# Second layer's down projection as seven block products, with weight blocks prepared during the first layer

## The chip, the cores and the metric

One core of one Trainium2 chip runs the whole kernel. The metric is the device time of one execution in microseconds (us). The kernel before was timed three times: 2796.79 to 2799.08 us, median 2798.24 us. Less is better. TensorE (PE) does the matrix products into PSUM, VectorE (DVE), ScalarE (ACT) and GpSimd (POOL) do elementwise work, SyncE (SP) issues the DMAs.

## The reference, cut to what matters

The reference is an encoder of two layers on 1024 positions of width 1024. Layer 0 has latent attention, layer 1 differential attention, and each ends with a gated MLP:

```
u = h @ w_up                       # 1024 -> 2 * 2816
u = conv over positions (width 3, depthwise) + bias
g, val = split(u)
x = x + (silu(g) * val) @ w_down   # 2816 -> 1024
```

After the second layer's MLP the output is `rmsnorm(x, final_norm_g)`. The change is about `(silu(g) * val) @ w_down` in both layers: in layer 1 its products change, and in layer 0 other work is set beside it. The weights `w_down` of both layers are inputs of the kernel.

## The kernel before, in words

**Layout.** Activations lie transposed: 128 features on the partitions, 1024 positions along the row. A matrix product of float32 accuracy is made of three TensorE passes over operands split into a high part (rounded to the engine's format) and a low part (the rest): high by high, high by low, low by high (`passes`). ACT makes a high part by a copy, POOL or DVE the low part by a subtraction. One matmul is 128 x 128 weights by 128 x 512 positions.

**The up projection** (`cycle` in each engine of `ffn_phase`) already works by seven block products, P1 to P7, of a 2 x 2 by 2 x 2 block scheme, for each of 22 pairs of tiles. Its result, the gated product y, goes tile by tile to DRAM (`ffn_products`), 22 tiles of 128 x 1024. The code names the last pair's products by `product_no(PAIRS - 1, ...)`.

**The down projection** (`project_down`, L1332 to L1334 for its passes) runs over 11 groups of two y tiles. In a group, TensorE makes 8 x 2 outputs (8 tiles of features, 2 halves of positions), each of 2 x 3 matmuls into one PSUM bank of eight (`DOWN_BANKS`, `NACC` = 8). It waits for the bank: output o needs the addition of output o - 8 (`acc_added`). DVE adds each output to the residual in SBUF (`add_down`, L1317). That is 176 outputs and 1056 matmuls in each layer. The fourth product of the last up pair (`fourth`) stands between the first two outputs.

**Order around it.** SP loads group g + 2 or later when the splits of a group have left the raw buffers (`fetch`). ACT's `step(g)` starts when group g - 2 is done on TensorE and splits two y tiles (`down_high_y`, L1129) and two weight tiles (`down_high_w`, L1134). POOL's `step(g)` makes the low parts (L1208, L1222). TensorE needs all of them for the group (`d_hi`, `d_lo`). Before the first group, SP loads the residual `x_out` from DRAM in eight DMAs (L1020), and DVE, after its last convolution and product of the up projection (`finish`), starts `add_down(0)`.

**End of layer 0.** In the last group, ACT and DVE also make the operands of the next layer's projections from the new residual: `unscaled_high` (L313) into `hh`, `unscaled_low` (L318) into `hl`, `unscaled_square` and `unscaled_add` for the norm, and `Ahead` loads and splits the first two weight tiles of the next phase. DVE's program has a `unscaled_low(m - 1)` behind the additions of tile m = 1, 2, 3, 4. A phase ends when all engines have come to its end.

**End of layer 1.** Each of the 16 additions of the last group is followed by a square on ACT (L1168), an addition of squares on POOL (L1235), and at the end a sum over partitions on TensorE (`norm_sum_halves`, L272): 12 matmuls of one column. Then DVE, ACT and DVE make the reciprocal root, and `final_norm_phase` scales and stores.

The engines' programs are written out by hand. Each engine runs its program in order. What holds it is the semaphore waits alone.

Of the kernel before, what the change touches and what calls it, by code (L numbers as in the profile page):

```python
# [18 lines left out]
F32 = mybir.dt.float32  # L19
# [6 lines left out]
P = 128  # L26
# [36 lines left out]
HX_AT = 28928  # L63
HX_HI_AT, HX_LO_AT = HX_AT, HX_AT + 56 * KB
# [768 lines left out]

def ffn_phase(nc, layer, x, x_out, x_dram, y_dram, up_dram, down_dram, vecs, cst, ones, nm, out_norm, unscaled, blocks, spaces,
              ahead):

    tag = f"ffn{layer}_"
    with ExitStack() as c:
# [59 lines left out]
        y_loaded = [sem(f"y_loaded{s}") for s in range(2)]  # L898
        down_loaded = [sem(f"down_loaded{s}") for s in range(2)]
        d_hi, d_lo = sem("down_hi"), sem("down_lo")  # L900
# [3 lines left out]
        last_use = [LastUse(d_hi, d_lo, 4 * (GROUPS - 1), acc_ready, lambda n: ADDS * (GROUPS - 1)) for s in range(2)]  # L904
# [7 lines left out]
        if unscaled:  # L912
            unscaled.squares_in(at("sq", [P, 3, SEQ], F32, RAW_AT), at("sq_more", [P, 3, SEQ], F32, PARTS_AT))
        else:
            sq = at("sq", [P, 3, SEQ], F32, RAW_AT)
            out_norm.sum_in(lambda k: x_out[:, k, :], [sq[:, 0, :], sq[:, 1, :]], sq[:, 2, :], ps[:, 0:QT],
                            sq_total=2 * KT)
# [50 lines left out]
        def _(sp):  # L968
# [14 lines left out]

            def load_down(g, s):
# [9 lines left out]
            def cycle(p, par, m):  # L994
                if is_last(p):
# [3 lines left out]
                    load_y(0, 0)  # L999
                    load_down(0, 0)  # L1000
# [15 lines left out]
            load_down(1, 1)  # L1016
            sp.wait_ge(prod, product_no(PAIRS - 1, "P5"))
            load_y(1, 1)
            for k in range(KT):
                sp.dma_start(x_out[:, k, :], x_dram[:, k, :]).then_inc(x_back[k], 16)  # L1020
            store_y(PAIRS - 1)
# [7 lines left out]
            with sp.Fori(1, (GROUPS - 1) // 2) as i:  # L1029
                fetch(2 * i, 0)  # L1030
                fetch(2 * i + 1, 1)
            fetch(GROUPS - 1, 0)
            if ahead:
                ahead.load(sp, last_use)

        @block.scalar
        def _(act):
# [43 lines left out]
            def cycle(p, par, m):  # L1081
# [22 lines left out]
                if is_last(p):  # L1104
                    down_high_y(0, 0, 1)
                need(act, prod, free(p, "A22"))
# [7 lines left out]
                if is_last(p):  # L1114
                    down_high_w(0, 0, 1)
                else:
# [25 lines left out]

            def step(g, s, m):
                if isinstance(g, int) and g == 0:
                    return
# [9 lines left out]
            if unscaled:  # L1155
# [2064 lines left out]
```

## Time and profile before

| | |
|---|---|
| median of three runs | 2798.24 us |
| profiled execution, its own time | 2799.92 us |
| its span | 2798.1 us |
| TensorE busy | 2715.1 us, 97% of the span |
| TensorE's mean granted clock | 0.991 |
| VectorE, ScalarE, GpSimd busy | 62%, 47%, 50% |
| DMA | 195.35 MB, mean 70 GB/s |
| down projection of layer 0 | 1159 to 1401 us of the span |
| down projection of layer 1 | from 2534 to 2775.7 us |

The profile gives one execution. Times are us from the start of the span. A matmul's own duration (about 390 ns in the rows) is longer than the distance to the next one, since matmuls overlap. The distance is what a matmul costs while TensorE has work.

### The profile page before, as it was taken

To read this page: it belongs to the slowest core of one execution; us is meant where nothing else is said; L and a number is where in the kernel's file an instruction comes from. 1 tells how busy PE (TensorE), PEld (TensorE's weight loads), DVE (VectorE), ACT (ScalarE), POOL (GpSimd) and SP (SyncE) were. 2 spreads that over 40 slices of the span, in tenths; PEclk is the share of its full clock that TensorE was granted. 3 is DMA by queue.
4 is the path that set the end of the run, shared out by engine and by line. 5 is a ranking of instruction groups with operands and counts; after the bars stand their busy time and mean duration, and the time that the engine had idled before them with its cause. 6 is when DMAs were issued, how large, how long until landed. Compare 5 with 4: busy or idle time off the path is not lost. (4 is left out here: it accounts for less than half of the span.)

```text
span 2798.1 us, 40653 instructions
## 1 busy us (share of the span) xinstructions
PE 2715.1 (97%) x13996; PEld 2263.8 (81%) x13996; DVE 1748.3 (62%) x2463; ACT 1314.0 (47%) x2035; POOL 1390.6 (50%) x1065
## 2 busy tenths in 40 slices
PE   8999999999989999999999999999898999999998
PEld 7788888887778888888878887887786888888886
DVE  6677777772764454555687777778428554455554
ACT  5577777772444444411245555555325444443112
POOL 1355555553687777644322222221247777775444
PEclk9999999999999999999999999999899999999999
DMA  3000000004122122522030000000321222125221
GB/s 140 23 11 10 7 7 7 18 1 160 51 91 90 68 90 90 203 91 105 30 115 31 31 31 31 31 23 23 158 106 38 90 90 86 71 105 196 95 85 60
DMA packets 54392, 195.35 MB, mean 70 GB/s; under 512 B 6545, under 2 KB 9873, under 8 KB 53777
## 3 DMA queue, kind: packets, MB, share of 16 engines
q1 hardware_dynamic: 54288, 193.95, 19.0%
q8 instruction: 68, 1.11, 0.2%
q14 instruction: 36, 0.29, 0.0%
HBM read 148.84 MB, written 45.09 MB: 69 GB/s over the span
## 5 line engine op out<-in xcount | busy, mean ns | idle before, releaser
L1332 PE MATMUL ffn_ps<-ffn_b,weights_hi 128*128 128x512 f32 x704 | 275.5, 391 | 11.7 <-ACT ffn_parts L1068 3.3
L1333 PE MATMUL ffn_ps<-ffn_b,weights_hi 128*128 128x512 f32 x704 | 274.4, 390 | 0.0
L1334 PE MATMUL ffn_ps<-ffn_b,weights_lo 128*128 128x512 f32 x704 | 274.4, 390 | 0.0
L1208 POOL TENSOR_TENSOR ffn_y_lo<-ffn_y_raw,ffn_y_hi 128x1024 fp32r<-128x1024 f32 x44 | 107.0, 2453 | 236.1 <-ACT ffn_y_hi L1129 236.1
L799 POOL TENSOR_TENSOR up_local_lo<-up_sums,up_local_hi 128x512 fp32r<-128x512 f32 x126 | 170.3, 1354 | 105.2 <-ACT up_local_hi L794 105.2
L409 POOL TENSOR_TENSOR weights_lo<-weights_raw,weights_hi 128x1024 fp32r<-128x1024 f32 (+2 forms) x64 | 124.4, 1949 | 192.6 <-ACT weights_hi L404 192.6
L2550 ACT ACTIVATE dif_p<-dif_s,dif_neg_max 128x1024 f32<-128x1024 f32 x128 | 142.4, 1115 | 143.3 <-DVE dif_neg_max L2755 143.3
L1332 PE MATMUL ffn_ps<-ffn_b,up_local_hi 128*128 128x512 f32 x504 | 196.3, 390 | 7.3 <-POOL up_local_lo L799 6.3
L1334 PE MATMUL ffn_ps<-ffn_b,up_local_lo 128*128 128x512 f32 x504 | 196.1, 389 | 0.0
L1333 PE MATMUL ffn_ps<-ffn_b,up_local_hi 128*128 128x512 f32 x504 | 196.1, 389 | 0.0
L1129 ACT ACTIVATE ffn_y_hi<-ffn_y_raw 128x1024 fp32r<-128x1024 f32 x44 | 44.2, 1051 | 315.0 <-PE ffn_ps L1334 315.0
L1317 DVE TENSOR_TENSOR x_second<-x_second,ffn_ps 128x512 f32<-128x512 f32 x176 | 120.3, 687 | 112.0 <-PE ffn_ps L1334 112.0
L2056 DVE TENSOR_REDUCE mat_row_max<-outer 128x1 f32<-128x1024 f32 x128 | 156.2, 1221 | 49.8 <-PE outer L420 48.1
L794 ACT ACTIVATE up_local_hi<-up_sums 128x512 fp32r<-128x512 f32 x126 | 78.9, 631 | 229.9 <-PE ffn_ps L1334 150.3
L1317 DVE TENSOR_TENSOR x_first<-x_first,ffn_ps 128x512 f32<-128x512 f32 x174 | 118.4, 686 | 103.9 <-PE ffn_ps L1334 103.9
L2755 DVE TENSOR_REDUCE dif_neg_max<-dif_s 128x1 f32<-128x1024 f32 x128 | 150.6, 1219 | 44.4 <-PE dif_s L2927 43.7
L1878 ACT ACTIVATE mat_pt_hi<-mat_turn 128x512 fp32r<-128x512 f32 x256 | 138.8, 594 | 79.0 <-PE mat_turn L2204 78.6
L1332 PEld LDWEIGHTS ffn_ps<-ffn_b,weights_hi 128*128 128x128 f32 x704 | 132.4, 188 | 42.9 <-issue 7.5
L1264 DVE SCALAR_TENSOR_TENSOR ffn_conv<-ffn_ps,vecs,ffn_conv 128x1023 f32<-128x1023 f32 x88 | 112.6, 1280 | 83.8 <-ACT ffn_conv L1053 83.8
L2073 DVE TENSOR_TENSOR mat_pt_lo<-mat_turn,mat_pt_hi 128x512 fp32r<-128x512 f32 x256 | 162.7, 677 | 2.3 <-ACT mat_pt_hi L1878 2.2
L1334 PEld LDWEIGHTS ffn_ps<-ffn_b,weights_lo 128*128 128x128 f32 x704 | 132.4, 188 | 27.6
L1333 PEld LDWEIGHTS ffn_ps<-ffn_b,weights_hi 128*128 128x128 f32 x704 | 132.4, 188 | 27.3
(420 smaller groups left out, 8169.4 us busy)
## 6 DMA issues: line engine op xcount, KB each, us to landing
weights_raw<-in_up SPq DMA_DIRECT2D x44, 512.0 KB, 3.7
up_raw<-in_up SPq DMA_DIRECT2D x44, 512.0 KB, 4.2
ffn_products<-ffn_conv SPq DMA_DIRECT2D x44, 512.0 KB, 2.6
ffn_y_raw<-ffn_products SPq DMA_DIRECT2D x44, 512.0 KB, 4.3
ffn_down_raw<-in_down SPq DMA_DIRECT2D x24, 512.0 KB, 6.8
weights_raw<-in_diff_qkv SPq DMA_DIRECT2D x23, 512.0 KB, 3.5
weights_raw<-in_down SPq DMA_DIRECT2D x20, 512.0 KB, 6.1
x_spill<-x_in SPq DMA_DIRECT2D x16, 512.0 KB, 3.9
```

The lines of the kernel that those rows point to most:

```text
L409: pool.tensor_tensor(w.lo[:], w.raw[:], w.hi[:].bitcast(F32), ALU.subtract).then_inc(w.lo_done, 1)
L799: pool.tensor_tensor(w.lo[name], w.block_raw(par, name), w.hi[name].bitcast(F32), ALU.subtract).then_inc(w.lo_done, 1)
L1264: dve.scalar_tensor_tensor(cv[:, 1:SEQ], pr[:, 0:SEQ - 1], vec(V_CONV_W + 2 * FT * 3 * layer, s, q), cv[:, 1:SEQ], ALU.mult, ALU.add).then ...
L1317: dve.tensor_tensor(xm, xm, bank(DOWN_BANKS[n % NACC]), ALU.add).then_inc(acc_added, 1)
L1332: pe.matmul(out, hi, x_hi, start=start, stop=False, skip_group_check=True)
L1333: pe.matmul(out, hi, x_lo, start=False, stop=False, skip_group_check=True)
L1334: return pe.matmul(out, lo, x_hi, start=False, stop=stop, skip_group_check=True)
L1878: act.activation(pt[:, 4 * half:4 * half + 4, (t % 2) * P:(t % 2 + 1) * P], turn_ps[half][:].rearrange("p (k m) -> p k m", m=P), ACT.Copy) ...
L2056: dve.tensor_reduce(row_max[:, col:col + 1], s_ps[t % 2][:], AX_X, ALU.max, negate=True).then_inc(max_ready, 1)
L2073: dve.tensor_tensor(pt_lo[b][part], turn_ps[half][:].rearrange("p (k m) -> p k m", m=P), pt_hi[b][part].bitcast(F32), ALU.subtract).then_i ...
L2550: act.activation((p0, p1)[m][t % 2][:], s_ps[m][:], ACT.Exp, bias=neg_max[:, col:col + 1], accum_out=total).then_inc(exp_done, 1)
L2755: dve.tensor_reduce(neg_max[:, col:col + 1], s_ps[m][:], AX_X, ALU.max, negate=True).then_inc(max_ready, 1)
```

## The change

**Layer 1, products.** The 22 y tiles are taken in six steps (`STEPS`): five of two pairs of tiles and one of one pair. In a step, the upper and the lower half of its tiles and the left and right half of the positions are the four blocks of y, and seven block products with seven blocks of weights replace the eight. A phase n of 42 is one product of one step; each makes four outputs q of `size` x 3 matmuls. TensorE's order is P1, P3, P2, P6, P5, P7, P4. POOL makes the four differences of y blocks (`difference`) and the low parts (`block_lo`), ACT the high parts (`block_hi`). DVE adds each output into the place of its kind of product (`place`): P1, P5, P6 have places of their own, the others lie in the residual. In the last step the places are combined (`combine`), 20 additions on DVE and 8 on POOL.

**Layer 1, weights.** They are not split there: SP loads the prepared high and low blocks of a phase, 512 KB each (half in step 1), in a ring of four (`load_weights`). In DRAM they lie by unit of 14 tiles, so a load takes runs of 1 KB.

**Layer 1, end.** 16 squares again. POOL adds ten of them into two, and TensorE sums these two and the last four: 24 matmuls.

**Layer 0.** Class `Prepare` makes the blocks in 11 rounds, one per group, of two units each. SP loads a unit's eight weight tiles in runs of 512 bytes, DVE makes four sums of 128 x 256, ACT the high part of 128 x 1792, POOL the low part of 128 x 1792, and SP stores both (0.92 MB each) and loads the next when the stores have landed. All of it stands in the engines' existing programs: DVE's sums of round 0 ahead of `add_down(0)`, those of round g + 1 in `add_down(g)` behind the additions of m = 3; ACT's and POOL's splits of round g at the end of `step(g)`; at the end ACT waits for all stores before its first `unscaled_high`.

The diff, cut:

```diff
+STEPS = ((0, 2), (4, 1), (6, 2), (10, 2), (14, 2), (18, 2))
+ORDER = ("P1", "P3", "P2", "P6", "P5", "P7", "P4")
+class Prepare:
+    def load(self, sp, g):
+        for j in range(2):
+            need(sp, self.stored[j], 32 * g)
+            for r in range(2):
+                for to, count, source in unit_source(self.source, 2 * g + j, r):
+                    sp.dma_start(self.raw[j][:, to:to + count, :], source).then_inc(self.loaded[j], 16)
+    def store(self, sp, g):
+        for j in range(2):
+            sp.wait_ge(self.lo_done, 2 * g + j + 1)
+            for z, part in enumerate((self.high[j], self.low[j])):
+                sp.dma_start(self.dest[2 * g + j, z], flat(part).bitcast(F32)).then_inc(self.stored[j], 16)
+    def sums(self, dve, g):
+        for j in range(2):
+            dve.wait_ge(self.loaded[j], 32 * g + 64)
+            dve.tensor_tensor(block(j, 8), block(j, 0), block(j, 4), ALU.subtract).then_inc(self.summed, 1)
+        for i, (to, a, b, op) in enumerate(...):      # three more for each j
+    def split_high(self, act, g):
+        for j in range(2):
+            act.wait_ge(self.summed, 8 * g + 7 + j)
+            act.activation(self.high[j][:], self.raw[j][:], ACT.Copy).then_inc(self.hi_done, 1)
+    def split_low(self, pool, g):
+        for j in range(2):
+            pool.wait_ge(self.hi_done, 2 * g + j + 1)
+            pool.tensor_tensor(self.low[j][:], ...)
...
 # SP, layer 0
             for k in range(KT):
                 sp.dma_start(x_out[:, k, :], x_dram[:, k, :]).then_inc(x_back[k], 16)
+            if prepare:
+                prepare.load(sp, 0)
             store_y(PAIRS - 1)
-            with sp.Fori(1, (GROUPS - 1) // 2) as i: ...
+            fetch(2, 0)
+            for g in range(GROUPS):
+                prepare.store(sp, g)
+                if g + 1 < GROUPS:
+                    prepare.load(sp, g + 1)
+                if g + 3 < GROUPS:
+                    fetch(g + 3, (g + 3) % 2)
+            ahead.load(sp, last_use)
+            prepare.all_stored(sp)
 # ACT, layer 0
             def step(g, s, m):
                 if isinstance(g, int) and g == 0:
+                    prepare.split_high(act, g)
                     return
...
                 down_high_w(g, s, m)
+                prepare.split_high(act, g)
             groups(act, step)
+            prepare.all_stored(act)
 # POOL, layer 0, end of step
+                prepare.split_low(pool, g)
 # DVE, layer 0
+                    if m == 3 and not end:
+                        prepare.sums(dve, g + 1)
...
             if unscaled:
+                prepare.sums(dve, 0)
+                groups(dve, lambda g, s, m: add_down(g))
                 return
 # DVE, layer 1
+            for n in range(PHASES):
+                s, name = n // 7, ORDER[n % 7]
+                last = s == len(STEPS) - 1
+                for q in range(4):
+                    o, to = 4 * n + q, place(name, q)
+                    if last and name == "P4":
+                        combine(to, place("P7", q), 5 + q)
+                        dve.wait_ge(combined, 17 + q)
+                    dve.wait_ge(acc_ready, o + 1)
...
+                if last and name == "P6":      # 8 combine
+                if last and name == "P5":      # 8 combine
 # PE, layer 1
+            for n in range(PHASES):
+                pe.wait_ge(weights_loaded[n % W_RING], 32 * (n // W_RING + 1))
+                pe.wait_ge(y_hi_done, n + 1)
+                pe.wait_ge(y_lo_done, n + 1)
+                for q in range(4):
+                    need(pe, acc_added, o - NACC + 1)
+                    for z in range(size):
+                        mm = passes(...)
+            pe.wait_ge(out_norm.sq_added, len(SQ_ADDED))     # ten
+            sum_squares(sq_part[:, 1, :], 1, first=True)
+            sum_squares(sq_part[:, 0, :], 0)
+            for n in range(2 * KT - 4, 2 * KT):
+                pe.wait_ge(out_norm.sq_ready, n + 1)
+                mm = sum_squares(sq_place(n), 0, final=n == 2 * KT - 1)
 # POOL, layer 1, last step
+                for q in range(4):
+                    pool.wait_ge(acc_added, last + 9 + q)
+                    pool.tensor_tensor(xm, xm, sum1[:, q, :], ALU.add).then_inc(c11_done, 1)
+                add_squares(SQ_ADDED[:6])
+                for q in range(4):
+                    pool.wait_ge(combined, 17 + q)
+                    pool.tensor_tensor(xm, xm, sum5[:, q, :], ALU.add).then_inc(c22_last, 1)
+                add_squares(SQ_ADDED[6:])
```

## Rows read from the trace of the kernel before

**Rows 1.** Page, busy time of each engine over the span.
```profile
PE 2715.1 (97%) x13996; PEld 2263.8 (81%) x13996; DVE 1748.3 (62%) x2463; ACT 1314.0 (47%) x2035; POOL 1390.6 (50%) x1065
```

**Rows 2.** Waits of PE, 1155 to 1405 us, then 2525 to 2798 us (total, times, longest).
```profile
PE dif_proj L418 <- PEq L3096: 2.5, 1, 2.5
...
PE fin_rstd L3032 <- PEq L3107: 1.6, 1, 1.6
PE ffn_ps L272 <- POOL ffn_sq L1235: 0.3, 1, 0.3
```

**Rows 3.** Timeline of DVE in layer 1's last group: start, us, instruction, idle before.
```profile
2766.26 0.69 DVE L1317 TENSOR_TENSOR x_second<-x_second,ffn_ps 128x512 f32<-128x512 f32 x1 [0.67 <-PE ffn_ps L1334]
2767.62 0.69 DVE L1317 TENSOR_TENSOR x_second<-x_second,ffn_ps 128x512 f32<-128x512 f32 x1 [0.67 <-PE ffn_ps L1334]
```

**Rows 4.** Timelines where layer 0's down projection begins: PE, SP, then DVE.
```profile
1159.03 0.39 PE L1332 MATMUL ffn_ps<-ffn_y_hi,ffn_down_hi 128*128 128x512 f32 x1
...
1163.11 0.39 PE L1332 MATMUL ffn_ps<-ffn_y_hi,ffn_down_hi 128*128 128x512 f32 x1
...
1157.64 4.18 SPq L1020 DMA_DIRECT2D x_first<-x_spill x8
...
1169.70 5.46 DVE L1317 TENSOR_TENSOR x_first<-x_first,ffn_ps 128x512 f32<-128x512 f32 x9
```

**Rows 5.** Timelines of ACT at two group starts, and of POOL for group 2's operands.
```profile
1183.79 2.01 ACT L1129 ACTIVATE ffn_y_hi<-ffn_y_raw 128x1024 fp32r<-128x1024 f32 x2 [14.76 <-PE ffn_ps L1334]
...
1205.46 2.01 ACT L1129 ACTIVATE ffn_y_hi<-ffn_y_raw 128x1024 fp32r<-128x1024 f32 x2 [17.77 <-PE ffn_ps L1334]
...
1184.93 4.78 POOL L1208 TENSOR_TENSOR ffn_y_lo<-ffn_y_raw,ffn_y_hi 128x1024 fp32r<-128x1024 f32 x2 [8.16 <-ACT ffn_y_hi L1129]
1189.67 4.74 POOL L1222 TENSOR_TENSOR ffn_down_lo<-ffn_down_raw,ffn_down_hi 128x1024 fp32r<-128x1024 f32 x2
```

**Rows 6.** Single lines: duration ns min/median/max, first and last start, form.
```profile
L1222 POOL TENSOR_TENSOR weights_lo<-weights_raw,weights_hi x20: 2386/2395/2422, 1172.0 to 2718.7; 128x1024 fp32r<-128x1024 f32 x20
L1235 POOL TENSOR_TENSOR ffn_sq<-ffn_sq x13: 1267/1292/1297, 2759.5 to 2775.8; 128x512 f32<-128x512 f32 x13
L1134 ACT ACTIVATE ffn_down_hi<-ffn_down_raw x20: 1042/1043/1048, 1150.2 to 2691.7; 128x1024 fp32r<-128x1024 f32 x20
L1168 ACT ACTIVATE ffn_sq<-x_second x16: 630/632/633, 2756.1 to 2776.5; 128x512 f32<-128x512 f32 x16
L2721 DVE TENSOR_TENSOR dif_rotated<-dif_rotated,dif_by_cos x32: 691/693/695, 1422.4 to 1933.6; 128x512 f32<-128x512 f32 x32
```

**Rows 7.** Page, DMA issues: KB each, median us from issue to landing.
```profile
ffn_products<-ffn_conv SPq DMA_DIRECT2D x44, 512.0 KB, 2.6
weights_raw<-in_mla_keys SPq DMA_DIRECT2D x8, 128.0 KB, 2.0
```

**Rows 8.** Windows: us, busy of PE, PEld, DVE, ACT, POOL, PEclk, DMA share, GB/s.
```profile
1170.00:1180.00 10.00, 10.00 (x46) 8.28 (x45) 7.53 (x13) 0.00 (x0) 6.77 (x3) 1.00 1.02 405
1227.30:1249.10 21.80, 21.80 (x98) 18.06 (x97) 11.04 (x17) 4.02 (x5) 9.48 (x4) 1.00 0.26 97
1379.50:1402.70 23.20, 21.77 (x97) 17.68 (x95) 20.36 (x22) 14.59 (x14) 5.76 (x2) 1.00 0.00 0
2778.00:2779.00 1.00, 1.00 (x6) 1.00 (x7) 0.00 (x0) 0.00 (x0) 0.00 (x0) 0.50 0.00 0
2779.00:2780.00 1.00, 1.00 (x5) 0.94 (x5) 0.00 (x0) 0.00 (x0) 0.00 (x0) 0.50 0.00 0
```

**Rows 9.** Timelines of DVE, ACT and POOL in layer 0's last group.
```profile
1385.59 3.07 DVE L318 SCALAR_TENSOR_TENSOR hl<-x_first,vecs,hh 128x1024 fp32r<-128x1024 f32 x1
...
1393.12 1.27 DVE L318 SCALAR_TENSOR_TENSOR hl<-x_first,vecs,hh 128x1024 fp32r<-128x1024 f32 x1
...
1382.99 1.15 ACT L313 ACTIVATE hh<-x_first,vecs 128x1024 fp32r<-128x1024 f32 x1 [19.78 <-DVE x_first L1317]
...
1385.17 5.76 POOL L409 TENSOR_TENSOR weights_lo<-weights_raw,weights_hi 128x1024 fp32r<-128x1024 f32 x2 [16.75 <-ACT weights_hi L404]
```

**Rows 10.** Timelines of PE and DVE where layer 1's down projection ends.
```profile
2775.35 0.39 PE L1334 MATMUL ffn_ps<-ffn_y_hi,ffn_last_lo 128*128 128x512 f32 x1
2775.84 1.05 PE L272 MATMUL ffn_ps<-ones,ffn_sq 128*128 128x1 f32 x8
2777.17 2.85 PE L272 MATMUL ffn_ps<-ones,ffn_sq 128*128 128x1 f32 x16 [0.28 <-POOL ffn_sq L1235]
...
2780.06 0.17 DVE L212 TENSOR_SCALAR final_norm_stat<-ffn_ps 128x8 f32<-128x8 f32 x1 [3.60 <-PE ffn_ps L272]
```

More of the change, by code:

```diff
@@ new lines, in quarter @@
+        def quarter(s, name):
+            size, buf = STEPS[s][1], tiles[s % 2]
+            upper, lower = buf[:, 0:size, :], buf[:, size:2 * size, :]
+            left, right = slice(0, HALF), slice(HALF, SEQ)
+            return {B11: upper[:, :, left], T3: upper[:, :, left], T1: upper[:, :, right], B21: lower[:, :, left],
+                    T4: lower[:, :, left], B22: lower[:, :, right], T2: lower[:, :, right]}[name]
+        BLOCK = {"P1": B11, "P3": B22, "P2": B21, "P6": T2, "P5": T1, "P7": T3, "P4": T4}
@@ L906, in b_part @@
+        LOWS = (0, T1, 1, T2, 2, T3, 3, T4, 4, 5, 6)
+        if prepared is None:
+            last_use = [LastUse(d_hi, d_lo, 4 * (GROUPS - 1), acc_ready, lambda n: ADDS * (GROUPS - 1)) for s in range(2)]
         def b_part(buf):
@@ L1112, in cycle @@
                     centre(1, p - 1, 1 - par)
-                if is_last(p):
+                if is_last(p) and prepared is None:
                     down_high_w(0, 0, 1)
+                elif is_last(p):
+                    block_hi(act, 1)
+                    block_hi(act, 2)
                 else:
@@ L1419, in project_down, with sum_squares @@
                         mm.then_inc(acc_ready, 1)
-            groups(pe, project_down)
             if unscaled:
+                groups(pe, project_down)
                 return
-            norm_sum_halves(pe, out_norm, ones, 2 * KT - 2, 2 * KT - 1)
+            for n in range(PHASES):
+                s, (hi, lo) = n // 7, parts_of(n)
+                size = STEPS[s][1]
+                pe.wait_ge(weights_loaded[n % W_RING], 32 * (n // W_RING + 1))
+                pe.wait_ge(y_hi_done, n + 1)
+                pe.wait_ge(y_lo_done, n + 1)
+                w_parts = weights[n % W_RING]
+                for q in range(4):
+                    o = 4 * n + q
+                    if o == 1:
+                        fourth(PAIRS - 1)
+                    if o in (2, 3, 4, 6):
+                        pe.wait_ge(*{2: (u2_done, PAIRS - 1), 3: (v_done, PAIRS - 1),
+                                     4: (conv_done[0], PAIRS), 6: (conv_done[1], PAIRS)}[o])
+                    need(pe, acc_added, o - NACC + 1)
+                    for z in range(size):
+                        mm = passes(bank(DOWN_BANKS[o % NACC]), w_parts[0][:, size * q + z, :], w_parts[1][:, size * q + z, :],
+                                    hi[:, z, :], lo[:, z, :], z == 0, z == size - 1)
+                    mm.then_inc(acc_ready, 1)
+            def sum_squares(squares, half, first=False, final=False):
+                for t in range(4):
+                    col = 4 * half + t
+                    mm = pe.matmul(out_norm.psum_sum[:, col:col + 1], squares[:, t * P:(t + 1) * P], ones[:, 0:1],
+                                   start=first and t == 0, stop=final and t == 3, skip_group_check=True)
+                return mm
+            pe.wait_ge(out_norm.sq_added, len(SQ_ADDED))
[4 more added lines that the diff above has]
+                mm = sum_squares(sq_place(n), 0, final=n == 2 * KT - 1)
+            mm.then_inc(out_norm.sq_summed, 1)
         return [bank(DOWN_BANKS[(2 * KT - 2 + half) % NACC]) for half in range(2)]
```

272 lines of the change are left out of this document (222 added, 50 removed).

## The prediction, made before the changed kernel was run

> **What bounds the kernel now.** I read the page's engine line first: TensorE is busy for 97% of the span [rows 1]. Then the waits of TensorE around both down projections: one wait of 2.5 us at a phase's start, 1.6 and 0.3 us at the end, and none inside [rows 2]. So here a matmul less is its distance to the next one less, and every other engine counts only where it makes TensorE wait. The distance: outputs of six matmuls follow each other every 1.36 us [rows 3], 0.227 us a matmul. A group of 16 outputs is 21.8 us, and ACT's group starts are 21.7 us apart [rows 5]. In such a group DVE has 11.0 us of work, ACT 4.0, POOL 9.5, the DMA a quarter of its time [rows 8]. That is the room into which layer 0 puts the preparation. But it has an order, and I follow that next.
>
> **Layer 1, TensorE.** The steps have sizes 2, 1, 2, 2, 2, 2, sum 11, and 7 products x 4 outputs x 3 passes: 924 matmuls in place of 1056. 132 x 0.227 = **-29.9 us**, if TensorE stays as full as now. DVE has 4 additions of 0.61 us (9 in 5.46 us, back to back [rows 4]) for a phase of 5.44 us, or 2.72 us in the small step: 2.44, just enough. POOL has per step 7 low parts and 4 differences of 2.4 us, 26 us of 38. A phase's weights are 1.05 MB, a step's tiles 2.1 MB: 9.5 MB in 38 us is 250 GB/s, and 405 GB/s were moved at a DMA share of 1 [rows 8]; the ring is three phases ahead, 16 us. Bounds 0 to +2 us for starved phases (the fourth weights stand behind the last y store, and land about when they are needed); I take 0. No row shows packets of 1 KB under load; see the rivals.
>
> **Layer 1, end.** Let T be the end of the last product, 2775.7 before; the column sums ended at T + 4.3 [rows 10]. In the last step DVE has, after P6's additions (T - 15.6), 8 combines, 4 additions, 8 combines, 4 additions, then four pairs of combine and addition: 32 instructions of 0.61 us, or 0.69 where one waits for the one before [rows 6]. That is T + 4.5, with no disturbance. The fourth c22 addition of POOL needs the last combine, T + 3.9, and behind it stand four additions of squares: 5 x 1.3 us [rows 6], so T + 10.4. TensorE waits for all ten additions before its first column sum. Then it has 24 matmuls where it had 12, recorded as 48 for 24. At half clock 11 records took 2 us [rows 8]: 48 take 8.7 us; at full clock 8 took 1.05 us: 6.3. The clock fell at about 2778, 2.3 us after the last product [rows 8, 10], and now TensorE does nothing for 10 us. DVE's combines read SBUF twice while POOL works. In the like place DVE's 128 x 1024 took 3.07 us while POOL was busy and 1.27 when it was not [rows 9]. I give each of the last four combines half a POOL instruction, +2.6 us. End T + 13 + 0.2 + 8.7 = T + 22: **+18 us**. Bounds: +12 (no disturbance, full clock) and +19 (each combine waits for a whole one).
>
> The Trainium skill, "SBUF — State Buffer", section "SBUF: two separate sides", says why: GpSimd and a DVE instruction with two SBUF inputs take a shared port in turn, whole instructions at a time. With it the end would be the upper bound, +19; the rows of 3.07 and 1.27 us agree with it.
>
> **Layer 0, start.** SP issues eight residual loads from 1157.6 to 1161.8, then, new, eight of 128 KB for round 0. The queue is full (share 1.02, 405 GB/s [rows 8]); 6.3 MB (two weight, two y, eight residual tiles) from 1155.5 last until 1171, and 1.05 MB more in runs of 512 bytes take 3.5 us (bounds 2.5 at the full rate, 5 at half). They land at about 1175.3. DVE used to start its additions at 1169.7 [rows 4]. Now it first waits for them and makes 8 sums of about 0.4 us (128 x 256; 0.69 for 512 [rows 6]): 3.2 us, so its first addition ends at 1179.2. TensorE needs it for the ninth output, at 1163.1 + 7 x 1.36 = 1172.6 [rows 4]: 6.6 us lost. Meanwhile ACT and POOL do round 0 before group 1. ACT: 128 x 1792 is 1.7 us (0.63 for 512, 1.04 for 1024 [rows 6]). POOL: 4.0 us (1.29 and 2.39 [rows 6]). The two low parts end at 1175.3 + 12.7 = 1188. Then POOL needs 9.5 us for group 1's operands [rows 5]: 1197.5. The stores of the second unit land 5.8 us after 1188: two of 0.92 MB are 4.5 us at 405 GB/s, and a store of 512 KB, landed in 2.6 us, has 1.3 beyond its transfer [rows 7]. Only then is the next load issued: 3.1 us (two issues, 1.8 as for the 128 KB loads [rows 7], 0.9 transfer). It lands at 1197, the sums end at 1200.1, and the addition of group 0's ninth output, which gives the next bank, at 1200.8. Group 1 starts at 1200.9, not 1183.7: **+17 us**. Bounds 14 and 20.
>
> **Layer 0, rounds.** Each round hangs on the one before: sums and splits 12.7, store 5.8, load 3.1, and 0.3 of wake-ups: 21.9 us, against TensorE's 21.8. Nothing of the eight banks' slack is left after group 1, so what a round takes above 21.8 is lost nine times. I take 22.6, since POOL, with 9.5 + 8.1 us a group, is often at work when DVE's sums come: **+7 us**. Bounds 21.8 (0; no gain, TensorE's own pace) and 25 (+29), with loads of 512 separate runs slow to issue or to land.
>
> The Trainium skill, "DMA: Bandwidth & Descriptors", section "Where 436 GB/s comes from", puts HBM traffic of a core at about 358 GB/s. By that estimate two stores and their loads would take 1 us longer and the sum 9 us more. The window above moved 405 GB/s, so the trace disagrees.
>
> **Layer 0, end.** Round 10's sums start 4 us before group 10 does, its stores land 18.6 us later: 14.6 us into the group. ACT waits for them before its first `unscaled_high`, which came 3.5 us into the group before [rows 8, 9]. DVE's `unscaled_low` behind m = 1 waits for that, and with it all later additions. Counting on (POOL's and ACT's splits of the next weights, queued behind the stores, come at 18.5, DVE has 10 additions, 4 lows of 1.27 and 3 additions of squares of 1.2 behind the first wait, and waits for ACT between them), DVE ends 32 us into the group, where it ended at 23.1: **+9 us**. Bounds +4 (stores early, by the free pace of DVE) and +11.
>
> **Sum.** -29.9 + 18 + 17 + 7 + 9 = +21. The profiled execution took 2799.92 us in all (span 2798.1), 1.7 above the median; on it 2821, and on the median of the runs, 2798.24, **2819 us**.
>
> **Rivals.** (a) *The rounds are hidden*: below 21.8 us a round, DVE's place behind m = 3 sets them; the stores of the last land about 9 us into group 10. +17 + 0 + 4 - 12 = +9, 2807 us. For it: the round is 21.9 by rows; against: no margin. (b) *The rounds are long*, 25 us: 17 + 29 + 10 - 12 = +44, 2842 us. For it: 512-byte runs of which no row exists, and the store, wait, load order; against: every piece is bounded by a row. (c) *Not slower*: the DMA engines deliver round 0's blocks before the residual, not behind it. Place: the first hole. Each us earlier than 1175 takes one off until DVE itself is free, 1169.7, and POOL then is done with group 1's operands at 1192 and the sums at 1194.7: the hole is 11.7 us. With (a) for the rest, 11.7 + 4 - 12 = +4, 2802 us, which no longer differs. It decides from a landing at about 1171. For it: the last residual load needs not be the last to land; against: full queue, later issue. All lower bounds together with it (end of layer 1 at +12) give -2, 2796 us. (d) *It does not do what it says*: weights in 1 KB packets at half the rate take 5.0 us and tiles 0.7 a phase, more than 5.44; TensorE would wait some 0.3 us a phase: 2830 us.
>
> **How the numbers follow.** Forecast 0.42, with a range of its own of 2809 to 2830; (a) 0.20, (b) 0.17, (c) 0.09, (d) 0.04; 0.08 remains for a gain that I don't see, down to the bare -30. From no change this kernel can be told by 0.2%, 5.6 us. Slower: forecast, (b), (d) and most of (a), 0.77; same: (c) and the rest of (a), 0.13; faster 0.10. The range 2790 to 2850 leaves out a tenth below and less above.
>
> **What would show it.** A wait of TensorE of about 6 us near 1173 and one of about 10 us before group 1; group starts in layer 0 at 22 to 23 us, with DVE waiting for a DMA at its sums; ACT waiting for DMA stores in group 10; 924 matmuls in layer 1 at 0.227 us with no gaps; TensorE idle for 10 to 13 us after the last product at a falling clock. The forecast is wrong if DVE's first wait is short, if the groups of layer 0 stay at 21.8 us, or if the column sums end within 10 us of the last product.

## The result: 41 us slower, and the profile after

The changed kernel takes 2839.49 us (median of 4 runs, 2838.42 to 2840.14) against 2798.34 (4 runs of the kernel before): ratio 1.0148, 95% interval 1.0136 to 1.0161. The forecast was 2819, inside a range of 2790 to 2850: the direction is right, the change is twice what was forecast. The profiled execution has a span of 2838.3 us, 40.2 more than before, at a mean granted clock of 0.978 in place of 0.991.

First the page of the changed kernel, the busy time of each engine. Against [rows 1] TensorE (PE) has 108 records less (132 products fewer, 24 records of column sums more), and POOL has 134 us more work. Then the waits of PE over the whole span (total, times, longest).

```profile
PE 2710.7 (96%) x13888; PEld 2257.6 (80%) x13888; DVE 1783.3 (63%) x2567; ACT 1345.6 (47%) x2055; POOL 1524.5 (54%) x1112
```

```profile
PE ffn_ps L1627 <- DVE x_first L1558: 25.2, 11, 9.1
PE ffn_ps L1742 <- POOL ffn_sq_part L1450: 12.7, 1, 12.7
...
PE dif_proj L419 <- PEq L3425: 8.1, 1, 8.1
...
PE ffn_ps L1627 <- DMA weights_lo<-down_blocks: 6.8, 2, 3.9
```

Where [rows 2] had one wait of 2.5 us around layer 0's down projection, there are now eleven on the residual's additions. Layer 1's down projection has two for weights, and its end has one of 12.7. Placed on the time axis, the 40.2 us of span are:

| stretch | before | after | change | forecast |
|---|---|---|---|---|
| start to the down projection of layer 0 | 1159.0 | 1157.6 | -1.5 | 0 |
| its group 1 starts, from there | 24.5 | 45.0 | +20.5 | +17 |
| nine rounds | 21.76 each | 22.75 each | +8.9 | +7 |
| last group's start to the attention's first projection | 24.4 | 34.5 | +10.1 | +9 |
| attention and up projection of layer 1 | 1129.8 | 1132.2 | +2.4 | 0 |
| down projection of layer 1, to its last product | 242.2 | 222.8 | -19.4 | -29.9 |
| last product to the end of the column sums | 4.3 | 23.1 | +18.8 | +18 |

(0.3 us lie behind the last row.) Each row is one profiled execution against one. In the twelve profiled executions of this document the start of layer 0's down projection lies between 1156.2 and 1159.0, and the attention with the up projection of layer 1 takes 1128.7 to 1133.9 us, so the first row and the fifth are within that scatter. I read each row in the timelines of the changed kernel.

*Layer 0, start.* The rows show DVE, then PE, then SP (start, us, instruction, idle before). They answer to [rows 4].

```profile
1175.18 0.43 DVE L895 TENSOR_TENSOR prepare_raw<-prepare_raw 128x256 f32<-128x256 f32 x1 [7.42 <-DMA prepare_raw<-in_down]
1176.76 0.42 DVE L895 TENSOR_TENSOR prepare_raw<-prepare_raw 128x256 f32<-128x256 f32 x1 [1.15 <-DMA prepare_raw<-in_down]
1177.10 2.09 DVE L899 TENSOR_TENSOR prepare_raw<-prepare_raw 128x256 f32<-128x256 f32 x6
1179.11 3.08 DVE L1558 TENSOR_TENSOR x_first<-x_first,ffn_ps 128x512 f32<-128x512 f32 x5
```

```profile
1179.85 0.80 PE L1627 MATMUL ffn_ps<-ffn_y_hi,ffn_down_hi 128*128 128x512 f32 x1 [8.51 <-DVE x_first L1558]
1202.56 0.77 PE L1627 MATMUL ffn_ps<-ffn_y_hi,weights_hi 128*128 128x512 f32 x1 [9.14 <-DVE x_first L1558]
```

```profile
1160.58 12.40 SPq L875 DMA_DIRECT2D prepare_raw<-in_down  x8
1173.02 0.69 SPq L1132 DMA_DIRECT2D ffn_products<-ffn_conv  x1
...
1190.46 6.20 SPq L875 DMA_DIRECT2D prepare_raw<-in_down  x4
```

DVE starts its first addition at 1179.11 (it was 1169.70), behind eight sums whose data came at 1175.2 to 1176.8. TensorE waits for the additions twice, 8.51 and 9.14 us; I call these the two holes. SP needs 12.40 us to issue the eight DMAs of round 0, and the last y store stands behind them. The row of 6.20 us merges the four DMAs of round 1 and is not issue time alone: SP issues two from 1190.46 to 1192.3, then waits until the second unit's stores have landed at 1195.72, and issues the other two from 1195.74 to 1196.7. They land at 1199.35.

*Layer 0, rounds.* The first rows are ACT's splits of two rounds. From 1201.51 to 1406.29 there are nine rounds, 22.75 us each. Then come windows, with the columns of [rows 8]: the first hole, one round, and three stretches at the half clock (0.50: 1.2 GHz in place of 2.4), at the two holes and at the attention's late start. In the round POOL is busy for 17.2 us of 22.8, and the DMA share is 0.84 in place of 0.26.

```profile
1201.51 3.29 ACT L904 ACTIVATE prepare_high<-prepare_raw 128x1792 fp32r<-128x1792 f32 x2 [15.54 <-DVE prepare_raw L899]
...
1224.61 3.30 ACT L904 ACTIVATE prepare_high<-prepare_raw 128x1792 fp32r<-128x1792 f32 x2 [16.02 <-DVE prepare_raw L899]
```

```profile
1170.00:1180.00 10.00, 1.50 (x7) 0.92 (x6) 3.67 (x10) 1.11 (x1) 0.00 (x0) 0.74 1.06 378
1205.50:1228.30 22.80, 22.80 (x101) 18.85 (x101) 12.67 (x24) 6.78 (x7) 17.20 (x7) 1.00 0.84 299
...
1174.80:1185.00 10.20, 5.15 (x12) 4.09 (x13) 7.65 (x16) 6.11 (x6) 4.33 (x2) 0.50 0.71 267
1198.70:1205.50 6.80, 2.94 (x7) 2.39 (x8) 6.12 (x14) 3.99 (x3) 2.21 (x1) 0.50 0.86 314
1437.60:1447.90 10.30, 6.10 (x15) 4.79 (x16) 9.16 (x12) 7.95 (x9) 0.00 (x0) 0.50 0.42 154
```

*Layer 0, end.* The rows show ACT's split of the last round, its wait for that round's stores, DVE behind it, and TensorE at the attention.

```profile
1406.29 3.29 ACT L904 ACTIVATE prepare_high<-prepare_raw 128x1792 fp32r<-128x1792 f32 x2 [15.54 <-DVE prepare_raw L899]
...
1423.19 1.15 ACT L314 ACTIVATE hh<-x_first,vecs 128x1024 fp32r<-128x1024 f32 x1 [12.09 <-DMA down_blocks<-prepare_low]
```

```profile
1424.38 1.28 DVE L319 SCALAR_TENSOR_TENSOR hl<-x_first,vecs,hh 128x1024 fp32r<-128x1024 f32 x1 [10.61 <-ACT hh L314]
```

```profile
1441.80 0.77 PE L419 MATMUL dif_proj<-hh,weights_hi 128*128 128x512 f32 x1 [8.10 <-PEq L3425]
```

*Layer 1.* The rows show TensorE's two waits for prepared weights, SP's issues ahead of the first one, and windows (the columns as above). The DMA share is 1.05 from 2574 to 2598, and behind each wait the granted clock is at its half for 3.4 us. SP issues nothing between 2579.0 and 2584.7: it waits until it can issue the last y store, and the fourth phase's weights stand behind that.

```profile
2597.04 0.50 PE L1627 MATMUL ffn_ps<-ffn_y_block_hi,weights_hi 128*128 128x512 f32 x1 [3.86 <-DMA weights_lo<-down_blocks]
2642.63 0.79 PE L1627 MATMUL ffn_ps<-ffn_y_block_hi,weights_hi 128*128 128x512 f32 x1 [2.89 <-DMA weights_lo<-down_blocks]
```

```profile
2578.11 0.84 SPq L1144 DMA_DIRECT2D ffn_tiles<-ffn_products  x2
2584.73 0.34 SPq L1132 DMA_DIRECT2D ffn_products<-ffn_conv  x1
2585.12 0.43 SPq L1154 DMA_DIRECT2D weights_hi<-down_blocks  x1
2585.60 0.51 SPq L1154 DMA_DIRECT2D weights_lo<-down_blocks  x1
```

```profile
2574.00:2598.00 24.00, 20.14 (x89) 16.39 (x88) 15.65 (x19) 8.01 (x10) 19.90 (x11) 1.00 1.05 400
2598.00:2602.00 4.00, 4.00 (x12) 3.09 (x12) 1.06 (x2) 1.15 (x2) 4.00 (x4) 0.57 1.09 384
...
2642.50:2646.00 3.50, 3.37 (x8) 2.70 (x9) 0.41 (x1) 0.00 (x0) 3.50 (x3) 0.51 1.09 386
```

*The end.* The rows show PE's last product and its column sums, then POOL, which works without a gap from 2792.99 to 2809.4, then DVE's last combine. They answer to [rows 10].

```profile
2796.38 0.39 PE L1629 MATMUL ffn_ps<-ffn_y_block_hi,ffn_weights_raw 128*128 128x512 f32 x1
2809.46 10.40 PE L1742 MATMUL ffn_ps<-ones,ffn_sq_part 128*128 128x1 f32 x48 [12.69 <-POOL ffn_sq_part L1450]
```

```profile
2792.99 4.74 POOL L1450 TENSOR_TENSOR ffn_sq_part<-ffn_sq_part 128x512 f32<-128x512 f32 x3 [11.75 <-ACT ffn_sq_part L1362]
2797.68 6.29 POOL L1460 TENSOR_TENSOR x_second<-x_second,ffn_sum 128x512 f32<-128x512 f32 x4
2803.94 5.47 POOL L1450 TENSOR_TENSOR ffn_sq_part<-ffn_sq_part 128x512 f32<-128x512 f32 x4
```

```profile
2800.59 1.04 DVE L1581 TENSOR_TENSOR x_second<-x_second 128x512 f32<-128x512 f32 x1
```

### The profile page after: what moved, and what is told of

It is laid out like the page before. It is cut to its first block and busy times, and to the rows that moved or that the text cites. A ratio compares the mean times of both kernels' runs of the same rounds, so it can differ in the third digit from the quotient of the medians.

```text
span 2838.3 us, 40499 instructions
## 1 busy us (share of the span) xinstructions
PE 2710.7 (96%) x13888; PEld 2257.6 (80%) x13888; DVE 1783.3 (63%) x2567; ACT 1345.6 (47%) x2055; POOL 1524.5 (54%) x1112
## 5 line engine op out<-in xcount | busy, mean ns | idle before, releaser
L2309 POOL TENSOR_TENSOR mat_passed<-mat_inv_sum 128x1 f32<-128x1 f32 x128 | 24.7, 193 | 253.3 <-DVE mat_inv_sum L2392 253.2
L2235 ACT ACTIVATE mat_probs<-outer,mat_shift 128x1024 f32<-128x1024 f32 x128 | 143.4, 1120 | 22.2 <-DVE mat_shift L2387 21.9
L419 PE MATMUL dif_proj<-hh,weights_hi 128*128 128x512 f32 x352 | 143.3, 407 | 8.2 <-PEq L3425 8.1
L2311 POOL TENSOR_SCALAR mat_probs<-mat_probs,mat_inv_sum 128x1024 f32<-128x1024 f32 x128 | 144.0, 1125 | 0.1
```

The source lines that it names most:

```text
L419: pe.matmul(out, w_hi, x_hi, start=start, stop=False)
L2235: act.activation(probs[t % 4][:], s_ps[t % 2][:], ACT.Exp, bias=shift[:, col:col + 1], scale=MLA_SCALE, accum_out=row_sum[:, col:col + 1]) ...
L2311: pool.tensor_scalar(probs[t % 4][:], probs[t % 4][:], inv_sum[:, col:col + 1], 1.0, ALU.mult, ALU.mult).then_inc(probs_scaled, 1)
```

## The experiments

My theory was that *order* costs the time, in three places. One raw buffer makes a ring of load, sum, split, store and the next load. The sums stand before the residual's additions. The weights stand behind a store in SP's program. The rivals are that the *load* (the bytes, POOL's work, the port) or the *short runs* of the DMAs cost the time wherever they stand. Each time is a median, and each diff is cut to the lines that matter, with "..." for what is left out. The kernel before, run beside them, took 2797.9 (experiments 1, 2, 3 and 6), 2798.4 (4, 5, 7 and 8) and 2797.8 us (9 and 10).

**1. The products alone.** Layer 0's down projection is as before. The blocks that layer 1 reads are copies of an operand of the attention, written to memory during the attention. The prepared sums are left out, so the output is not the reference's, but the work of layer 1 is the same.

```
             for g in range(GROUPS):
-                prepare.store(sp, g)
-                if g + 1 < GROUPS:
-                    prepare.load(sp, g + 1)
...
+                for i in range(8):
+                    fill(8 * h - 8 + i)
```

> Layer 0 as in the kernel before (no loads, sums, splits or stores of weight blocks); layer 1 by the seven block products of the changed kernel. Its weight blocks are 44 plain copies of an operand of the attention, stored to DRAM in the attention phase, where the DMA queue is mostly idle; so the output is not the reference's. Theory 'order' (the loss is in three places of layer 0 and two of layer 1, each named by a wait): layer 1 gives 30 us by fewer matmuls, loses 7 to late weights and 3 to a half clock behind them, and 19 at its end: about 1 us under the kernel before, 2797 us. The forecast's own terms for layer 1 (-30 + 18) would give 2786 us. If the extra loss over the forecast sat in layer 0 alone, this run would show 2786.

Measured: 2799.42 us, ratio 1.0006 (0.9996 to 1.0015). That is 2 us above the 2797 expected, and 13 above the 2786 of the forecast's own terms. The preparation costs 40 us, and the seven products without it gain nothing. TensorE keeps the waits below, and what 132 matmuls give is given back. Waits of PE from 2500 us on:

```profile
PE ffn_ps L1731 <- POOL ffn_sq_part L1443: 12.7, 1, 12.7
PE ffn_ps L1616 <- DMA weights_lo<-down_blocks: 6.4, 2, 3.9
```

**2. The preparation alone.** The kernel before with the rounds in its layer 0; nothing reads them.

```
+            if prepare:
+                prepare.load(sp, 0)
             store_y(PAIRS - 1)
...
```

> The preparation in layer 0 alone, as in the changed kernel; layer 1 as before (the stored blocks are not read). Theory 'order': start 20, rounds 9, end 10, and 2 in the attention's beginning at half clock: 2798 + 42 = 2840 us. The forecast's terms for layer 0 (17 + 7 + 9) would give 2831 us.

Measured: 2838.26 us, ratio 1.0147 (1.0130 to 1.0164). So the two parts add up (40.4 + 1.5 = 41.9 us against 41.2). The forecast had 33 us for the preparation and 12 us of gain for the products, so 7 us of its miss are in the preparation and 13 in the products. Waits of PE, 1150 to 1445 us:

```profile
PE ffn_ps L1432 <- DVE x_first L1413: 26.5, 11, 10.3
PE dif_proj L418 <- PEq L3197: 8.1, 1, 8.1
```

**3. A second raw buffer.** Odd rounds have raw and low tiles of their own, so a load waits for the stores of the round before the last and not of the last. The high tiles are still shared: ACT now waits for their stores. The instructions and the bytes are the same.

```
-                need(sp, self.stored[j], 32 * g)
+                need(sp, self.stored[j], 32 * (g - 1))
...
+            need(act, self.stored[j], 32 * g)
...
-                if g + 1 < GROUPS:
-                    prepare.load(sp, g + 1)
+                if g + 2 < GROUPS:
+                    prepare.load(sp, g + 2)
```

> The changed kernel with a second pair of raw buffers for the odd rounds, so that the loads of a round no longer wait for the stores of the round before; same bytes, same instructions, same places in the programs of DVE, ACT and POOL. Theory 'order' (a round's sums wait for the stores of the round before): groups of layer 0 at TensorE's own 21.8 us in place of 22.75 (-9), group 1 no longer waits for the second sums but for POOL (-4), the last stores land about 9 us into group 10 in place of 15 (-5): 2821 us. Rival 'load' (299 GB/s of DMA and 17.4 us of POOL work in a group slow it by themselves): groups stay at 22.7, at most the start changes, 2835 us or more.

Measured: 2825.70 us, ratio 1.0103 (1.0086 to 1.0120), 14 less than the change. The load stays and the time goes, so in the rounds it is the ring. ACT's splits are now 21.6 us apart, and eight of TensorE's nine groups are back at 21.76 us:

```profile
1241.25 3.29 ACT L910 ACTIVATE prepare_high<-prepare_odd_raw 128x1792 fp32r<-128x1792 f32 x2 [13.40 <-DVE prepare_odd_raw L904]
...
1262.83 3.29 ACT L910 ACTIVATE prepare_high<-prepare_raw 128x1792 fp32r<-128x1792 f32 x2 [13.13 <-DVE prepare_raw L904]
```

It is 5 us above what I expected. ACT's wait for the last stores (12.06 us at 1409.28) and the late first additions stayed. And the first of the nine groups takes 24.54 us: TensorE works its first 5.69 us at the half clock (0.50 from 1194.70 to 1204.90), behind its wait of 6.80 us, and half of that is lost.

**4. The start moved too.** The same as 3, with round 0's sums behind DVE's first four additions, and group 1's operands split before round 0.

```
+                    if m == 1 and isinstance(g, int) and g == 0:
+                        prepare.sums(dve, 0, 0)
...
+                if isinstance(g, int) and g == 1:
+                    prepare.split_high(act, 0, 0)
```

> The double-buffered split (odd rounds have raw and low tiles of their own) with its start moved as well: in the change VectorE makes round 0's sums before the residual's first addition and ScalarE and GpSimd split round 0 before group 1's operands; here the sums stand after the first four additions, and group 1's operands are split first. Theory order (places in the programs and in SyncE's queue cost the time, not the bytes or the engines' load): group 1 starts about 10 us earlier than with the double buffer alone, rounds at the old 21.8 us, so 2814 to 2818 us. Rival load (the added loads, stores and POOL's work cost it wherever they stand): the split's work only moves into the rounds, 2824 us or more.

Measured: 2818.69 us, ratio 1.0070 (1.0053 to 1.0086): 7 less again, 0.7 above the range expected and 5 under the rival's. Group 1 starts 33.8 us into the down projection (43.0 in experiment 3, 45.0 in the change), and the group behind it again takes 24.1. TensorE's two waits for the residual fell from 8.5 and 9.1 us to these, with the same instructions on every engine:

```profile
1180.75 0.80 PE L1640 MATMUL ffn_ps<-ffn_y_hi,ffn_down_hi 128*128 128x512 f32 x1 [2.51 <-DVE x_first L1570]
1192.81 0.76 PE L1640 MATMUL ffn_ps<-ffn_y_hi,weights_hi 128*128 128x512 f32 x1 [4.82 <-DVE x_first L1570]
```

**5. No last round.** The change without round 10's loads, sums, splits and stores. Layer 1 reads an earlier round's blocks in its place, so its numbers differ and its work does not.

```
-                prepare.split_high(act, g)
+                if not (isinstance(g, int) and g == GROUPS - 1):
+                    prepare.split_high(act, g)
```

> The change without its eleventh and last round of loads, splits and stores (the last round's four blocks are left out; the second layer reads the blocks of an earlier round in their place, so its numbers differ and its amount of work does not). Theory: what lengthens the end of the first layer's down projection (34.4 us against 24.2 from the last group's start to the attention's first projection) is that ScalarE and VectorE wait there for the last stores; without them about 10 us go: 2829 to 2831 us. Rival (the end is late because GpSimd's split stands ahead of the norm's work, or because the round before drains into it): at most 3 us go, 2836 us or more.

Measured: 2829.10 us (2823.90 to 2829.76), ratio 1.0103 (1.0086 to 1.0120): 10.4 less, as expected. From the last group's start to the attention are 24.5 us again. The run takes out the splits together with the stores and does not part them; that the wait was for the stores is read from ACT's row of 12.09 us above. PE reaches the attention without the long wait:

```profile
1430.62 0.71 PE L419 MATMUL dif_proj<-hh,weights_hi 128*128 128x512 f32 x1 [2.62 <-PEq L3434]
```

**6. Weights first.** In layer 1, SP issues the fourth weights before the second tiles and the last y store, and later weights before the next step's tiles; the waits are the same ones.

```
+                sp.wait_ge(prod, product_no(PAIRS - 1, "P4"))
+                load_weights(3)
                 sp.wait_ge(lo_done, block_no(PAIRS - 1, "A22"))
                 load_tiles(1)
                 store_y(PAIRS - 1)
...
+                    load_weights(n)
                     if n % 7 == 0 and n // 7 + 1 < len(STEPS):
```

> The changed kernel with another order on SP in layer 1: the fourth phase's weights ahead of the tiles of step 1 and the last y store, and at each step the phase's weights ahead of the next step's tiles. Theory 'order' (the weights were late because they stood behind these loads): both waits of TensorE (3.9 and 2.9 us) go or nearly go, and the half clock behind each: 2830 to 2833 us. Rival 'short runs' (1 KB runs are slow by themselves): waits stay, 2839 us.

Measured: 2830.55 us, ratio 1.0117 (1.0100 to 1.0134): 8.9 less, by SP's order alone. The fourth phase's weights are now issued at 2578.81 and land at 2593.77 (2585.12 and 2596.99 in the change). The runs of the DMAs are as short as they were, so by themselves they don't make TensorE wait. What is left of the waits for weights:

```profile
PE ffn_ps L1627 <- DMA ffn_weights_lo<-down_blocks: 0.7, 1, 0.7
PE ffn_ps L1627 <- DMA weights_lo<-down_blocks: 0.2, 1, 0.2
```

**7. TensorE kept at work in its last wait.** 52 products (`FILL`) are written into a bank that has been read; nobody uses them.

```
+            for i in range(FILL):
+                pe.matmul(bank(DOWN_BANKS[1]), w_parts[0][:, 0, :], hi[:, 0, :], ...)
             pe.wait_ge(out_norm.sq_added, len(SQ_ADDED))
```

> The change, with 52 products of 0.227 us written to a bank that is already read, in the wait of TensorE for GpSimd's last partial square sum; nothing else differs. In the changed kernel TensorE waits 12.7 us there, its clock is at 0.50 from 10 us before the 48 column-sum records, and these take 10.4 us. Theory clock (the low level behind the wait is a cost of its own): the records take about 6.3 us, the whole 4 to 6 us less than the change, 2834 to 2836 us. Rival (the records are bound by their own form and not by the clock): 10.4 us again and 2839 us; if the fillers run past GpSimd's sum, 2840 or more.

Measured: 2837.96 us (2837.09 to 2838.55), 1.5 less in the medians and 3.1 in the spans, against 4 to 6. The profile bears the theory out, the medians only in part: the 48 records take 6.94 us in place of 10.40, but start 0.4 later, and nothing behind them became faster.

```profile
2809.89 6.94 PE L1743 MATMUL ffn_ps<-ones,ffn_sq_part 128*128 128x1 f32 x48 [1.12 <-POOL ffn_sq_part L1451]
```

**8. Combining earlier.** Eight of the 20 combines moved out of DVE's last three phases.

```
+                    if last and name == "P7":
+                        dve.wait_ge(acc_added, o + 1)
+                        combine(place("P4", q), to, 5 + q)
+                if last and name == "P1":
+                    dve.wait_ge(acc_added, 4 * n + 4)
+                    for q in range(4):
+                        combine(place("P6", q), place("P1", q), 0)
...
```

> The change with two groups of VectorE's additions among the sums moved earlier in the last step of the second layer: sum 6 plus sum 1 directly behind P1's products instead of behind P6's, and the fourth quarter plus the seventh's in P7's phase instead of P4's. Theory: GpSimd's last square sum, for which TensorE waits 12.7 us, is late because VectorE does its extra additions in the last three phases in a row; 5 us of them leave the path: 2833 to 2836 us, with TensorE's wait near 7 us. Rival (GpSimd's own additions of sum 5 and the ten square sums in its program order bound it): 2838 or more, wait 11 us or more.

Measured: 2839.01 us (2837.13 to 2840.67), no difference that the medians can tell; the profiled span is 3.0 less. TensorE's wait is 10.7 us: not the 7 expected, and just under the rival's 11. DVE's last combine ends at 2797.5 in place of 2801.6, which is 3.3 nearer to the last product (that ends 0.9 sooner too). But the wait fell by 2.0 only, because POOL is at work from 2790.2 without a gap, 5.0 + 5.8 + 5.5 us. In the change it was the same 16.4 us, from 2793.0 on. What the edit moved is POOL's start, which waits for ACT's squares behind DVE's combines of P5. So DVE's lateness sets when POOL starts, and POOL's own work sets the rest: the rival holds for most of the wait.

```profile
2790.21 5.03 POOL L1450 TENSOR_TENSOR ffn_sq_part<-ffn_sq_part 128x512 f32<-128x512 f32 x3 [9.86 <-ACT ffn_sq_part L1362]
2795.20 5.84 POOL L1460 TENSOR_TENSOR x_second<-x_second,ffn_sum 128x512 f32<-128x512 f32 x4
2801.01 5.48 POOL L1450 TENSOR_TENSOR ffn_sq_part<-ffn_sq_part 128x512 f32<-128x512 f32 x4
```

**9. Four repairs together.** These are 4, 6, 8, and 7 with 24 products.

> The whole change with four repairs together: the double-buffered split with its later start, the second layer's weights issued before its operand tiles and y store, VectorE's two groups of sums moved earlier, and 24 filling products in TensorE's last wait. By their separate runs (2818.7 with the split repaired; 8.9 less by the weights' order, 0.5 and 1.5 less by the last two) 2806 to 2809 us if each is a place of its own. Rival (they share their time, as the second layer's start now comes with other queues): 2812 us or more. Either way it stays above the kernel before.

Measured: 2807.79 us (2804.93 to 2810.63, 7 runs), ratio 1.0037 (1.0025 to 1.0049). By the separate runs it should be 2818.7 - 8.9 - 0.5 - 1.5 = 2807.8. So the places are separate ones, though the last two terms are within the scatter, and that the sum is hit to 0.1 is luck. It is still slower than the kernel before. PE at the end: the wait is down to 5.3 us, but the 24 products end that much before the sums, and the sums run at the half clock again.

```profile
2765.22 5.60 PE L1765 MATMUL ffn_ps<-ffn_y_block_hi,ffn_weights_raw 128*128 128x512 f32 x24
2776.14 10.40 PE L1759 MATMUL ffn_ps<-ones,ffn_sq_part 128*128 128x1 f32 x48 [5.32 <-POOL ffn_sq_part L1460]
```

**10. The products alone, repaired.** This is 1 with 6, 8, and 7 with 24 products; the blocks are copies as in 1.

> The seven products alone with the same repairs but for the split's: no rounds in the first layer (the second layer reads constant blocks, written to memory in the attention between the layers, so its numbers differ and its work does not), weights first, sums earlier, 24 filling products. Theory: of the 29.9 us that 132 products are worth, 18.8 go at the end of layer 2 and about 10 in late weights and the clock behind them; with the latter back and 2 to 4 of the former, 2785 to 2789 us, 10 to 13 below before. Rival (the late weights only hide another wait, such as the operands' splits): 2793 us or more.

Measured: 2786.79 us (2784.23 to 2788.79), ratio 0.9960 (0.9946 to 0.9974). So the block products gain 11 us, once their weights come for nothing. Preparing them costs 2839.5 - 2799.4 = 40 as written, and 2807.8 - 2786.8 = 21 repaired.

## Why the prediction was half right

**Layer 1's products: the step that failed.** The prediction took "Bounds 0 to +2 us for starved phases [...]; I take 0". The measured term is 10.5 us. The matmuls did come at 0.227 us while TensorE had its operands, but it waited 6.8 us for weights and worked at the half clock for 3.4 us behind each of the two waits. Half of that time is lost, 3.4 us together, which makes some 10. Experiment 6 gave 8.9 back by order alone. The working compared means, 250 GB/s wanted and 405 to be had, where the single item counts. From 2574 to 2598 the DMA engines are full (share 1.05, 400 GB/s) with weights, residual, tiles and the y store, and the fourth phase's weights are issued behind all of these. The text even says that they "stand behind the last y store, and land about when they are needed"; TensorE waited 3.9 us for them. The second wait is the same mistake at a step's change, where 2.1 MB of tiles are issued ahead of a phase's weights. Rival (d) had waits in layer 1 too, but 0.3 us in every phase and by 1 KB runs; the change shows two waits, and another order of the same DMAs takes nearly all of them away.

**The clock behind stalls: missing in the sum, 3.4 us of the 10.5.** The sum prices the half clock at the end of layer 1 alone, and not the 3.4 us lost behind the two waits for weights. In layer 0 the half clock showed no price of its own. Behind the first hole TensorE worked 5.15 us at the half clock, and then waited 9.14 us all the same. Behind the second it worked 2.94 us so, but the next groups are paced by the ring: the first two of the nine take 23.25 and 22.23 us, together two rounds of 22.74. Without the ring it has a price, 2.8 us in experiment 3. Behind the attention's late start TensorE worked 6.10 us at the half clock, but the 2.4 us of that stretch can't be put down to it: in experiment 2, which has the late start, the stretch takes 1128.8 us, 1.0 less than before, and in experiment 5, which has not, 1133.9.

**Layer 0, start: mechanism right, short by 3.5.** In absolute time the forecast is close. DVE's first addition was to end at 1179.2 and ended at 1179.8. Group 1 was to start at 1200.9 and started at 1202.56. On the way, the second unit's stores took 7.0 us from issue to landing (1188.76 to 1195.72) where the working had 5.8, and the load behind them 3.6 where it had 3.1. The rest is that the down projection began 1.5 us earlier in this execution and the data for round 0 did not come earlier, so the first hole was 8.5 us and not 6.6.

**Rounds: number right, in part by luck.** They took 22.75 us against 22.6, and experiment 3 shows the ring as the cause. But the 0.7 us above the chain of 21.9 was put down to POOL being at work when DVE's sums come. In each of rounds 1 to 10 of the changed kernel, sums and splits take 12.0 to 12.1 us from the landing of the second unit's load, less than the 12.7 of the working, so POOL was not in their way. The stores behind them take 6.9 to 7.1 us in place of 5.8, and in rounds 2 to 10 the load behind those 3.5 to 4.1 in place of 3.1. Two sizes were too small, and an allowance for something else covered them.

**Layer 0, end: right.** It is +10.1 against +9, by the wait named (ACT for the last stores, which landed 15.8 us into the group, forecast 14.6), and experiment 5 takes 10.4 away.

**Layer 1, end: right in sum, by errors that cancel.** It is +18.8 against +18: the sums began 12.7 us behind the last product (forecast 13.2) and took 10.40 us in place of 8.7. The working had DVE's combines as the long chain, the last one ending 6.5 us behind the last product. It ended at 4.9: three of the last four took 1.03 to 1.04 us, where the working had 0.69 and half a POOL instruction on top. The long chain is POOL's, 16.4 us without a gap, and its own instructions were stretched too: three of the four additions in the row of 6.29 us took 1.72 each, the fourth, behind DVE's last addition, 1.26. The sum of the Trainium skill's rule that the prediction named ("SBUF — State Buffer", section "SBUF: two separate sides") was +19, as close, but its chain, each combine waiting for a whole POOL instruction, isn't what these rows show. The disturbance itself stands clearest in experiment 3, DVE then POOL: two sums of a round took 4.02 us while POOL worked, against 0.43 each in the first rows above, where it did not.

```profile
1235.43 4.02 DVE L900 TENSOR_TENSOR prepare_odd_raw<-prepare_odd_raw 128x256 f32<-128x256 f32 x2
```

```profile
1234.22 4.96 POOL L1481 TENSOR_TENSOR weights_lo<-weights_raw,weights_hi 128x1024 fp32r<-128x1024 f32 x2
```

The errors add up, in the order of the headings: 10.5 for layer 1's products, 3.5, 1.9 and 1.1 for layer 0, 0.8 for the end, and then 2.4 for the attention stretch, -1.5 before the down projection and 0.3 behind the last row. That is 19.0 of the 19.2 us between 40.2 and 21. The scatter of runs is about 1.5 us to either side, so terms of that size are not settled one by one. The time measured lies nearest to rival (b), 2842 us, but its mechanism, rounds of 25 us, did not come. The split between waits and clock in layer 1 rests on the windows; only at the end of layer 1 was the clock tried apart (experiment 7).

## What to carry to other kernels

Work moved under a full TensorE costs what its places cost, not what its bytes and instructions do: of the 40 us of preparation, 19 went by a second buffer and another place of the same instructions. What remains, 21 us, stands at the two ends. In experiment 9, group 1 starts 9.4 us later than before, the group behind it takes 2.3 more, and the last group's end 6.8 more. Price a moved stream at its start, its end and each change of step, with what is ahead of it in the queue there; a mean rate that fits hides a late first item. A saving on TensorE at the end of a program reaches the time only if what stands behind it has less to do too. Here the end gave back 19 us, 12.7 of waiting for POOL and the rest in twice as many column sums at the half clock.

## What the runs showed of the hardware

- SP can stand at the issue of a DMA while the DMA engines are full. The eight loads of 128 KB of round 0 (512-byte runs, share 1.03 from 1160.5 to 1173) took 12.40 us to issue, one of them 5.70 alone, where the eight residual loads of 512 KB just before them took 4.34. It isn't the 512-byte runs alone: in layer 1, at a share of 1.05, one load of weights in 1 KB runs took 3.68 us to issue.
- Filling TensorE's last wait gave the clock back only where it lasted nearly to the end. With 1.12 us idle in front, the 48 records took 6.94 us; with 5.32 us idle behind 24 filling products they took 10.40, as with no filling.
- One core alone moved 400 GB/s over 24 us (2574 to 2598). The Trainium skill's limit of about 358 GB/s, which the prediction named ("DMA: Bandwidth & Descriptors", section "Where 436 GB/s comes from"), is not seen here either.
- On a row of the page, the stores of the high blocks (896 KB) land after 3.7 us (median), those of the low blocks, issued 0.4 us later, after 6.4. The ring waited for the later ones.
